# A three-layer transformer stack on one core: the first transfers in another order and shape, query pieces in other banks, all weights repacked in DRAM

## What is computed

```python
def reference(x, ...):
    h = x                                         # (1, 256, 1024)
    hn = rmsnorm(h, norm_mix[0])                  # x * rsqrt(mean(x*x) + eps) * g
    qkv = hn @ w_qkv                              # 1024 -> 3 * 1024, 16 heads of 64
    s = q_chunk @ k_band * HEAD_DIM ** -0.5 + rel_table[:, clip(rel)]   # bias by distance
    p = softmax(where(key_pos >= 0, s, -1e30))
    h = h + (p @ v_band) @ w_o
    h = h + relu(rmsnorm(h, norm_mlp[0]) @ w1[0]) ** 2 @ w2[0]
    # then the recurrent layer with its MLP, and the second block, all float32
```

## Time and profile before

| | |
|---|---|
| median of 3 runs | 1002.58 us (1002.58 to 1002.81) |
| profiled execution | 1003.32 us, of which the span is 1001.5 us |
| PE busy | 994.0 us, 99% of the span |
| DVE, ACT busy | 683.1 us, 555.9 us |
| DMA | 184.80 MB, mean 185 GB/s |

### The profile page before, as it was taken

The page is one execution under the profiler, slowest core; times in us unless marked ns, Lnnn a source line. Parts: engine busy times, 40 slices in busy tenths (PEclk is TensorE's granted clock), DMA queues, the critical chain, the costliest instruction groups (busy, mean ns, idle before and its releaser), DMA issues.

```text
span 1001.5 us, 14148 instructions
## 1 busy us (share of the span) xinstructions
PE 994.0 (99%) x5620; PEld 859.1 (86%) x5620; DVE 683.1 (68%) x925; ACT 555.9 (56%) x804; POOL 34.5 (3%) x37
## 2 busy tenths in 40 slices
PE   9999999999999999999999999999999999999997
PEld 7988788888889988888888888888888788888886
DVE  5777676665667897756666767665668867666564
ACT  6678654444446866444444655545467655545453
POOL 1000010000002300000000100000010010000000
PEclk9999999999999999999999999999999999999999
DMA  9943375565563545655665565765625455765621
GB/s 335 311 158 127 127 262 190 192 212 184 170 207 107 191 154 202 232 190 168 205 209 174 169 215 192 223 202 185 202 86 147 130 197 169 240 210 168 210 85 43
DMA packets 124559, 184.80 MB, mean 185 GB/s; under 512 B 3162, under 2 KB 103182, under 8 KB 124366
## 3 DMA queue, kind: packets, MB, share of 16 engines
q1 hardware_dynamic: 122304, 176.70, 53.5%
q0 software_dynamic: 1728, 6.60, 1.8%
q10 hardware_dynamic: 462, 0.60, 0.2%
HBM read 182.81 MB, written 1.07 MB: 184 GB/s over the span
## 4 chain that ended last, share of the span: by engine, by line
PE 97%; DVE 2%; ACT 0%; issue 0%; POOL 0%; DVEq 0%; POOLq 0%
PE bank L1560 37%; PE bank L1506 28%; PE bank L1513 14%; PE bank L1495 4%; PE bank L1497 3%; PE bank L1498 3%; PE bank L1586 1%; PE bank L1735 1%; PE bank L1681 1%; PE bank L1711 1%; PE bank L1695 1%; DVE w_lo L829 1%; DVE work L1006 0%; PE bank L1880 0%; PE bank L1881 0%; PE bank L1882 0%
## 5 line engine op out<-in xcount | busy, mean ns | idle before, releaser
L829 DVE TENSOR_TENSOR w_lo<-raw,w_hi 128x2048 fp32r<-128x2048 f32 x164 | 374.0, 2289 | 129.4 <-ACT w_hi L426 128.4
L426 ACT ACTIVATE w_hi<-raw 128x2048 fp32r<-128x2048 f32 x164 | 311.6, 1908 | 33.9 <-PE bank L1560 31.0
L1506 PE MATMUL bank<-xT,w_hi 128*128 128x512 f32 x1216 | 294.0, 390 | 0.0
L1506 PEld LDWEIGHTS bank<-xT,w_hi 128*128 128x128 f32 x1216 | 224.6, 188 | 43.8
L1513 PEld LDWEIGHTS bank<-xT,w_lo 128*128 128x128 f32 x1216 | 159.8, 191 | 8.4
L1513 PE MATMUL bank<-xT,w_lo 128*128 128x256 f32 x1216 | 162.3, 282 | 0.0
L1560 PE MATMUL bank<-w_hi,z_hi 128*128 128x512 f32 x472 | 153.2, 393 | 0.2
L1560 PE MATMUL bank<-w_lo,z_hi 128*128 128x512 f32 x472 | 152.0, 390 | 0.0
L1560 PE MATMUL bank<-w_hi,z_lo 128*128 128x512 f32 x472 | 151.7, 390 | 0.0
L470 ACT ACTIVATE work<-bank 128x256 f32<-128x256 f32 x152 | 49.8, 379 | 170.6 <-PE bank L1513 170.6
L1560 PEld LDWEIGHTS bank<-w_hi,z_lo 128*128 128x128 f32 x472 | 88.6, 188 | 18.9
(11 more groups left out here) (213 smaller groups left out, 770.9 us busy)
## 6 DMA issues: line engine op xcount, KB each, us to landing
raw<-in_w SPq DMA_DIRECT2D x64, 1024.0 KB, 5.3
raw<-in_f_gate SPq DMA_DIRECT2D x22, 1024.0 KB, 5.3
raw<-in_f_up SPq DMA_DIRECT2D x22, 1024.0 KB, 6.0
raw<-in_f_down SPq DMA_DIRECT2D x22, 1024.0 KB, 4.9
raw<-in_w_in SPq DMA_DIRECT2D x11, 1024.0 KB, 5.6
raw<-in_w_qkv SPq DMA_DIRECT2D x9, 1024.0 KB, 9.0
raw<-in_w_o SPq DMA_DIRECT2D x4, 1024.0 KB, 4.9
raw<-in_rec_w_o SPq DMA_DIRECT2D x4, 1024.0 KB, 5.0
```

The lines of the kernel that those rows point to most:

```text
L426: e.activation(*by_channel(n, w_hi[n % RING], raw[n % RAW]), ACT.Copy).then_inc(hi_done, 1)
L829: e.tensor_tensor(low_, here, high, ALU.subtract).then_inc(lo_done, 1)
L1506: e.matmul(bank[i], whi[:, k, b * P:(b + 1) * P], xT[:, k, :, :].rearrange("p b s -> p (b s)"), start=(k == 0), stop=False, skip_group_che ...
```

## The change

**Host side.** All weight matrices are packed into one array `pieces` of 167 x 128 x 2048, in the order of use; each piece is one contiguous 1 MB with 8 KB per partition, and its transfer one source row per partition. The number of bytes and the ring of four buffers stay. The array `x_turned` has the first norm's gain (8 columns) and x already turned, `cols` has all gains and biases already as columns, and `er` has the widened table.

**Start.** SP issues x turned in four parts (blocks 0; 1; 2 and 3; 4 to 7) into `x_home`, piece 0 in four quarters, pieces 1 to 3 in halves. PE turns neither x nor vectors, and `WARM` is 34. x as rows (`h`) is loaded only after piece 5, for the squares and the later residual sum, followed by half the bias (1 MB, straight from `er`); the other half comes after piece 8.

**Middle.** `qk_piece(0)` to `(2)` go to banks 4, 5 and 6, and so need not wait until the values have left banks 1 to 3; `qk_piece(3)` waits for all of these. `spread(L0)` moves on PE from before `qk_piece(0)` to after the fourth block of `qk_piece(1)`. On ACT the squares come after `hi(5)`, and the four exits of the values (line 604 before) after the squares. On DVE `variance` and `diags` come after `lo(5)`.

The core of the diff:

```diff
-HALVED = 3
-WARM = 32
+HALVED = 4
+WARM = 34
-    pieces = [d_src(A["w_qkv"][:, 2 * D:3 * D], i * 2 * P) for i in range(4)]
+    pieces = [A["pieces"][n] for n in range(TOTAL)]
...
+    def qk_bank(m):
+        return bank[4 + m] if m < 3 else bank[1 + m % 3]
...
+            here = slice(X_ENDS[i], X_ENDS[i + 1])
+            e.dma_start(x_home[:, here], A["x_turned"][:, here]).then_inc(x_in[i], 16)
...
+                if n == N_QK + 1:
+                    e.dma_start(h, A["x"].rearrange("(t p) c -> p t c", p=P)).then_inc(h_in, 16)
+                    bias_part(0)
+                elif n == N_QK + 4:
+                    bias_part(1)
...
     def scalar(e):
+        hi_quarter_of(0)
+        hi_quarter_of(1)
+        hi_quarter_of(2)
+        hi_quarter_of(3)
+        e.dma_start(cols, A["cols"]).then_inc(in_cols, 16)
...
-        hi(3)
+        e.wait_ge(sp_step, 2)
+        e.activation(sp[2], sp[1], ACT.Exp).then_inc(sp_exp, 1)
+        hi(4)
+        hi(5)
         for half in range(2):
             for t in range(T):
                 square(L0, half, t)
-        hi(4)
         for t in range(T):
             e.wait_ge(v_closed, t + 1)
...
-        hi(5)
         hi(6)
...
     def vector(e):
-        variance(L0)
-        diags(L0)
...
         lo(4)
         small_steps()
         lo(5)
+        variance(L0)
+        diags(L0)
         spread(L0)
         lo(6)
...
     def tensor(e):
-        for g in range(2):
-            rows = VEC_ROWS[g]
-            e.wait_ge(vec_in[g], 16)
-            e.transpose(bank[0][:, g * P:g * P + rows], vec_rows[0:rows, g, :], ident[0:rows, 0:rows]).then_inc(
-                vec_turned, 1)
-        for k in range(2):
-            turn(L0, k)
...
-        spread(L0)
...
-            e.wait_ge(v_done, [2, 3, 4][min(m, 2)])
-            if m >= 3:
+            if m == 3:
+                e.wait_ge(v_done, 4)
+            elif m >= 6:
                 e.wait_ge(qk_left, m - 2)
...
-        qk_piece(1)
+        qk_piece(1, (lambda: spread(L0), nothing))
         qk_piece(2, (lambda: scores(a1, 0), nothing))
```

More of the change, by code:

```diff
@@ L383, in x_part, with bias_part @@
         def x_part(i):
-            here = slice([0, 2 * P, HALF][i], [2 * P, HALF, D][i])
-            e.dma_start(h[:, :, here], A["x"].rearrange("(t p) c -> p t c", p=P)[:, :, here]).then_inc(x_in[i], 16)
+            here = slice(X_ENDS[i], X_ENDS[i + 1])
+            e.dma_start(x_home[:, here], A["x_turned"][:, here]).then_inc(x_in[i], 16)
+        def bias_part(i):
+            heads = slice(i * N_HEADS // 2, (i + 1) * N_HEADS // 2)
+            rows = bass.AP(tensor=A["er"].tensor, offset=A["er"].offset + heads.start * ER,
+                           ap=[[1, P], [ER, N_HEADS // 2], [1, S]])
+            e.dma_start(bias[:, heads, :], rows).then_inc(in_bias[i], 16)
         x_part(0)
@@ L422, in hi @@
         def hi(n):
-            e.wait_ge(landed[n % RAW], 16 * (n // RAW + 1 + sum(m <= n and (n - m) % RAW == 0 for m in BY_HEAD)))
+            e.wait_ge(landed[n % RAW], 16 * (n // RAW + 1))
             if n >= RING:
@@ L446, in square @@
             else:
-                for part in ((2,) if half else (0, 1)):
-                    e.wait_ge(x_in[part], 16)
+                e.wait_ge(h_in, 16)
             i = 2 * half + t
@@ L588, in scalar @@
             x_hi(L0, k)
-        for kk in range(2):
-            hi_part(2, kk)
-        hi(3)
+        for n in (2, 3):
+            for kk in range(2):
+                hi_part(n, kk)
+        e.wait_ge(sp_step, 2)
+        e.activation(sp[2], sp[1], ACT.Exp).then_inc(sp_exp, 1)
+        hi(4)
+        hi(5)
         for half in range(2):
@@ L1115, in vector @@
             x_lo(L0, k)
-        e.wait_ge(in_rel, 16)
-        e.tensor_copy(er[0:N_HEADS, 0:FAR], table[0:N_HEADS, 1:FAR + 1]).then_inc(er_near, 1)
-        e.tensor_copy(er[0:N_HEADS, FAR:ER], bcast(table[0:N_HEADS, FAR:FAR + 1], [0, ER - FAR])).then_inc(er_far, 1)
-        for kk in range(2):
-            lo_part(2, kk)
-        lo(3)
-        variance(L0)
-        diags(L0)
+        for n in (2, 3):
+            for kk in range(2):
+                lo_part(n, kk)
+        e.wait_ge(in_cols, 16)
         sp0().then_inc(sp_step, 1)
@@ L2010, in shape_constants, with piece_rows, u_src, d_src @@
     return {"rope": rope, "mask2": mask, "pool_m": pool_m}
+def piece_rows(w):
+    def u_src(w, c):
+        return w[:, c:c + 2 * P].reshape(KB, P, 2 * P).transpose(1, 0, 2)
+    def d_src(w, r):
+        return w[r:r + 2 * P, :].reshape(2, P, D).transpose(1, 0, 2)
+    def ffn_pieces(ups, down, pairs):
+        order = [u_src(m, 0) for m in ups]
+        for p in range(1, pairs):
+            order += [u_src(m, p * 2 * P) for m in ups]
+            order.append(d_src(down, (p - 1) * 2 * P))
+        return order + [d_src(down, (pairs - 1) * 2 * P)]
+    def pool_src(i):
+        return w["w_in2"][i * 4 * P:(i + 1) * 4 * P, 768:1280].reshape(4, P, 4 * P).transpose(1, 0, 2)
+    def q_src(i):
+        both = w["w_in2"].reshape(KB, P, 1280).transpose(1, 0, 2)
+        return np.stack([both[:, :, (2 * n + i) * P:(2 * n + i + 1) * P] for n in range(KV_2)], axis=1)
+    def heads_src(i):
+        tops = [(n * 4 + 2 * i) * HD for n in range(KV_2)]
+        return np.concatenate([w["w_out"][o:o + P].reshape(2, HD, D).transpose(1, 0, 2) for o in tops], axis=0)
+    pieces = [d_src(w["w_qkv"][:, 2 * D:3 * D], i * 2 * P) for i in range(4)]
+    pieces += [u_src(w["w_qkv"], m % 2 * D + m // 2 * 2 * P) for m in range(8)]
+    pieces += [d_src(w["w_o"], i * 2 * P) for i in range(4)]
+    pieces += ffn_pieces([w["w1"][0]], w["w2"][0], FM0.pairs)
+    pieces += [u_src(w["w_in"], m * 2 * P) for m in range(8)]
+    pieces += [d_src(w["rec_w_o"], i * 2 * P) for i in range(4)]
+    pieces += ffn_pieces([w["w1"][1]], w["w2"][1], FM1.pairs)
+    pieces += ffn_pieces([w["f1_gate"], w["f1_up"]], w["f1_down"], FF1.pairs)
+    pieces += [u_src(w["w_in2"], 512), q_src(0), pool_src(0), pool_src(1), q_src(1)]
+    pieces += [d_src(w["w_out"], (2 + i) * 2 * P) for i in range(2)]
+    pieces += [heads_src(i) for i in range(2)]
+    pieces += ffn_pieces([w["f2_gate"], w["f2_up"]], w["f2_down"], FF2.pairs)
+    assert len(pieces) == TOTAL
+    return np.stack([np.ascontiguousarray(x).reshape(P, PIECE) for x in pieces])
 def kernel(**inputs):
@@ L2039 @@
     }
+    arrays["pieces"] = piece_rows(arrays)
+    for name in WEIGHTS:
+        del arrays[name]
     arrays.update(shape_constants())
```

222 lines of the change are left out of this document (92 added, 130 removed).

## The result

| | kernel before | changed kernel |
|---|---|---|
| median of the runs on the same chip | 1002.75 us | 1005.02 us |
| profiled execution, and its span | 1003.32, 1001.5 us | 1006.67, 1004.8 us |

The ratio is 1.0022, with a 95% interval of 1.0013 to 1.003: slower by 2.3 us (1.3 to 3.0), where 1.0 us faster was forecast.

The account below looks back on a forecast made before the run. PE, busy for 99% of the span, was taken as the bound. T = 5.2 + 21.75 + 0.1 + 0.6 = 27.65 gave a gain of 28.72 - T = 1.07 us: 1002.25 profiled, median stated as 1001.6, range 1000.3 to 1003.3.

Parts of the forecast that it names:

- T: Start of qk_piece(0), the first query product, after the values; forecast at 27.65 us.
- First product: PE's first value product at the start: forecast at 5.2 us (5.0 to 5.6), 1.1 us sooner than before.
- The clock term: Time added to the value products by PE's half clock at the start: taken as 0.6 us, rising near 6.4.
- rival 1: Value products: half clock as long as now; T 28.65 to 29.25, median 1002.5 to 1003.1; chance 0.34.
- The supply holds: During the value products, 2.1 MB land before piece 1's first half is needed at about 11.3 us.
- T + 8.64 for the spread, T + 9.33 for the copy: Query pieces: the moved spread starts on PE at T + 8.64; DVE's copy of rms at T + 9.33.
- No third wait: At qk_piece(2): lo(6) ends at T + 11.95, just when it starts; hi(6) done about 34, needed by 37.3.
- qk_leave(1)` at T + 14.67 and a wait of 2.0 us before the scores: DVE's queue behind the spread puts its second query exit at T + 14.67, so PE waits 2.0 us.
- Splits: DVE's splits of pair 0, needed by the scores: end 2.05 us after the second query exit, at T + 16.72.
- From there on the same work: After DVE's second query exit both kernels do the same work, so the end moves by 28.72 - T, 1.07 us.
- Pieces of 8 KB: Weight transfers with 8 KB per partition: no gain, no cost; bounds 0 to 0.3 us either way, first 2 MB.
- rivals, 4: Start to spread: h behind six pieces lands late, deciding from 32 us on; at 35.5, 1005.1; chance 0.05.

Follow-up runs that it names:

- e2: Changed kernel with DVE's 24 small steps of the bias moved from between lo(4) and lo(5) to beside the first MLP; 1004.53 us.
- e3: Changed kernel with hi(6) and hi(7) before the value exits on ACT and lo(6) before the spread on DVE; 1002.55 us.
- e4: Changed kernel with h fetched ahead of piece 5 and ACT's squares ahead of hi(5); 1005.24 us.
- e6: Changed kernel with the small steps beside the first MLP and the split orders of ACT and DVE both turned; 1002.38 us.
- e7: Kernel of e6 with 42 products of zeros instead of 34; 1002.32 us.
- e13: Changed kernel with the small steps beside the first MLP and DVE's lo(6) before the spread, ACT's order unchanged; 1002.41 us.
- e12: Changed kernel with ACT's order alone turned: hi(6) and hi(7) before the four value exits; 1005.02 us.
- e5: Changed kernel with the second half of piece 0 in one transfer of 4 KB runs instead of two quarters; 1004.55 us.
- e9: Changed kernel with the edits of e2, e3 and e5 together; 1001.62 us.
- e10: Kernel of e9 with the first half of piece 0 in one transfer as well; 1001.80 us.
- e14: Kernel of e9 with x's third part cut in two, the second of them behind piece 1's first half; 1001.23 us.
- e8: Changed kernel with the rows of the transposed x padded to a multiple of 64 bytes; 1004.64 us.
- e11: Kernel of e9 with the small steps left where the change has them; 1001.85 us.
- e1: Kernel before with its weights packed piece by piece, 8 KB per partition, and nothing else changed; 1003.08 us, ratio 1.0004.

## Why the prediction was wrong, step by step

The chain of the forecast is right in its form: T, then a chain on DVE, then the same work as before. Its terms, in the profiled execution of the changed kernel, whose second scores came 4.4 us later than forecast:

- **First product**: 5.62 for 5.2, just outside its bounds of 5.0 to 5.6. Plus 0.4. The gain of 0.3 from the smaller first transfer did not come: ACT had the first quarter at 4.8, no sooner than the 4.7 of before, and from 3 to 4 us the queues moved 188 GB/s instead of the 369 by which that gain was counted. What made the product 0.72 us sooner is that ACT no longer waits for `cols`.
- **The clock term** was taken as 0.6. The products kept to half the clock until 9, 8 products or 1.6 us, which was rival 1's number. Plus 1.0. But this term does not stand alone, as the next point shows.
- **"The supply holds"** failed. Piece 1's first half was rounded from 11.98 on, and its products start at 13.18, 0.67 after the last one before it where 0.23 is usual: plus 0.5 on top of a slow clock. With a fast clock the pause grows to 1.7 to 2.2 us (e2, e3, e4, e6, e7, e13) and T is 29.4 to 30.0, against 27.65. So the landing alone puts T there, and a fast clock would not have saved the forecast: the step that failed is this one, with the price "0 to 0.3 us" for the cutting. The 383 GB/s at 8 us, from which I took that the cut costs nothing, were those of the kernel before with another cut; in the changed kernel 6 to 8 us ran at 171. By 9 us 1.8 MB had been moved on SP's queue, before 2.2. The forecast dismissed by that row what the Trainium skill says (DMA: Bandwidth & Descriptors, Rules for kernel authors), which asks for at least 1 MiB per DMA. The runs agree with it in direction: by 9 us 1.76 to 1.86 MB had been moved with piece 0 in quarters, 1.97 to 2.01 with its second half in one transfer. Where the rest of the shortfall against the kernel before (2.27 MB) comes from stays open.
- **T + 8.64 for the spread, T + 9.33 for the copy**: T + 8.72 and T + 9.36. Right.
- **"No third wait"**: in this execution there was one, 1.65 us to the next start, because `hi(6)` was forecast for 34 and ended at 40.7. Two things were missed: `h` landed at 28.8 instead of 25.2, and on DVE the variance is queued behind `lo(4)`, the small steps and `lo(5)`. That came to 35.15 where I had counted only squares to diagonals. I priced the chain behind the spread by DVE's order and the chain ahead of it as if DVE were free. In the medians this step costs nothing that was measured (e4, e12), but once T comes sooner it takes the gain away (e5).
- **`qk_leave(1)` at T + 14.67 and a wait of 2.0 us before the scores**: T + 14.62 and 1.97 in e12_act_order; with the third wait T + 16.13. Right, and the largest term of all, worth 2.1 us in e13_dve_order. The forecast had it in its sum.
- **Splits**: `z_lo` ended 2.05 us after `qk_leave(1)` began before, 2.45 now. Plus 0.4. It is 2.0 in the kernels with the small steps moved (e2, e6, e7, e9, e10, e13, e14), and 2.45 in e3, e4, e5, e8, e11 and e12. Why is open; the trace names no later releaser.
- **From there on the same work**: not quite. In the profiles of the changed kernel, of e8_aligned and of e12_act_order the granted clock falls to half for 3.41 us after the wait. From the end of `z_lo` to the second scores it was 9.1 us in the changed kernel (48.19 to 57.27) and 8.5 before (45.44 to 53.98), as in all the kernels whose clock stayed up. Plus 0.5. No step allowed for it. It costs no more because the forecast's second wait, ahead of the turned weights, is there in the variants of the changed kernel whose clock stayed up (0.72 us at 54.32 in e2_small_late, for 0.8 forecast) and gone in these three: the slow products fill it.
- **Pieces of 8 KB: nothing.** Right as far as e1 can tell: 1.0004, and 1 lies inside its interval.

In sum for this execution: 0.4, 1.0 and 0.5 make T later by some 2.0 (29.61 for 27.65), then 1.5 for `hi(6)`, 0.4 for the splits, 0.5 for the clock: 4.4 us, as measured. For the medians the account is less complete: the forecast was 1001.6 and 1005.0 was measured, 3.4 us. The later T is 1.4 to 2.0 of it (e12_act_order, the changed kernel), splits and clock some 0.9 more, 0.2 is the median of before in these runs. What the rest is, the single profiled executions don't settle, but the lists of runs point at the clock. Executions with a mean granted clock of 0.997 and less are the longer ones (e12_act_order: 5 of 11, 1005.2 against 1004.5; e3_splits_first: 2 of 10, 1004.3 against 1002.5). The six kernels whose trace has a long wait before the scores all have them, 2 to 5 of 10 or 11; e3_splits_first has two and e7_all one, the other seven variants none, and the kernel before has one among more than a hundred.

Of the rivals, 4 named the right sign, and with 1005.1 even the time, by the wrong mechanism, so that was luck: `h` landed at 28.8, under the 32 from which it was to decide, the spread still came at T + 8.72, and e4_h_sooner gave nothing. Rival 1 had the right price for the clock, and would have come to 1003.1 at most. A rival was missing that says: the new order fetches in time for PE's order of work, and the first two megabytes come slower than they did.

## What to carry to other kernels

When a stage of PE is made to start sooner, follow the queue of every engine that serves the next stage from its first instruction, not from the point where the trace of before has it waiting; here the helper was fully counted behind the spread and not at all ahead of it. An engine that will wait for PE should have its next independent work put ahead of the waiting instruction: one line moved on DVE gave 2.1 us, nearly all of the 2.3 that the change had cost. Don't judge the supply of a new order of transfers by the rate that the old order reached: here the first two megabytes came slower, and how much slower varied between executions. And look for the one instruction from which the rest of the span takes the same time in all variants; here the end of the last split told within 0.2 us what each edit gave in its trace, the half microsecond of the clock apart.

## What the hardware did that I had not expected

- The DMA engines were busy for 82% of the stretch from 6 to 8 us and moved 171 GB/s; in the kernel before they were busy throughout and moved 353. Eight more executions with the same cut of piece 0 had 174 to 225. With piece 0 in two halves it was 268; the remainder of some 85 GB/s is unexplained.
- Neither 32 nor 34 nor 42 products of zeros made the time of the first high clock certain: the profiled executions had it at 9.83 (before) and 5.10 us (e1_packed_only) with the same order of work, and at 8.98 (changed kernel), 5.54 (e3), 4.26 (e13) and 5.89 us (e7_all, 42 products) after nearly the same work.
- Waits of PE of 2.2 us to the next start were followed by 3.41 us at half the clock in three profiled executions, and by none in two others (e4_h_sooner, e5_halves) with a wait as long. In those three the clock had first risen at 9.0 to 9.4 us, in the two at 4.7 and 4.9. Whether this is a connection was not tried. A wait of 1.82 us (e2_small_late) was followed by none in its profiled execution, though 4 of its 10 runs have a granted clock of 0.997.
